# One visit of transposes per expert instead of two in a two-layer decoder trunk

## The reference

```python
xt = v.reshape(-1, d)                       # 512 tokens x 1024
scores = softmax(xt @ w_router)             # 16 experts in 4 groups
# one group per token (sum of its two best scores), then the two best experts in it
for e in range(16):
    hidden = silu(xt @ w_gate[e]) * (xt @ w_up[e])      # 1024 -> 512
    y = y + combine[:, e:e + 1] * (hidden @ w_down[e])  # 512 -> 1024
```

## Time and profile before

| | |
|---|---|
| median of 3 runs | 1138.19 us (1136.5 to 1138.63) |
| the profiled execution's own time | 1138.1 us |
| its span, first to last instruction | 1135.8 us |
| mean granted TensorE clock | 0.997 |
| busy: PE, DVE, ACT, POOL | 1108.5, 894.3, 750.2, 131.6 us |
| DMA | 286.28 MB, mean 252 GB/s over the span |
| expert loops | about 300 to 530 us and 820 to 1050 us of the span |

### The profile page before, as it was taken

One profiled execution on the slowest core, in us unless ns is written; L12 is line 12 of the kernel. 1 busy time (PEld: TensorE's weight loads), 2 busy tenths in 40 slices (PEclk: granted clock), 3 DMA queues, 4 the chain that ended last, 5 costly groups with the idle time before them and its releaser, 6 DMA issues.

```text
span 1135.8 us, 16852 instructions
## 1 busy us (share of the span) xinstructions
PE 1108.5 (98%) x5722; PEld 886.3 (78%) x5722; DVE 894.3 (79%) x1226; ACT 750.2 (66%) x957; POOL 131.6 (12%) x91
## 2 busy tenths in 40 slices
PE   9999999999999999999999999999999999999996
PEld 7888877767888888888788865766888888888785
DVE  6483488358999999999876479638999999999886
ACT  7383322347778787878655469446787878888665
POOL 0000000001212122120000000001221212121000
PEclk9999999999999999999999999999999999999999
DMA  9473222425999999999761310423999999999632
GB/s 367 170 286 149 84 75 81 179 111 210 364 379 375 381 370 387 375 384 376 286 230 46 112 38 20 167 97 136 336 376 380 380 379 370 389 374 387 258 141 74
DMA packets 50595, 286.28 MB, mean 252 GB/s; under 512 B 9321, under 2 KB 9597, under 8 KB 21358
## 3 DMA queue, kind: packets, MB, share of 16 engines
q1 hardware_dynamic: 37086, 250.93, 57.8%
q0 software_dynamic: 13456, 34.65, 8.3%
HBM read 271.38 MB, written 30.41 MB: 266 GB/s over the span
## 4 chain that ended last, share of the span: by engine, by line
PE 84%; DVE 8%; ACT 4%; DMA 2%; issue 1%; SPq 0%; DVEq 0%; ACTq 0%; POOLq 0%
PE psum L568 79%; PE psum L939 2%; DVE arena L2662 2%; ACT whi L1384 2%; DMA arena<-vscr,cur 1%; DVE arena L2675 1%; PE psum L980 1%; DVE wlo L1946 1%; DMA h<-x_dram 1%; DVE wlo L1942 1%; ACT ahi L1384 1%; PE psum L850 1%; DVE h L2496 0%; DVE h L2503 0%; DVE arena L2148 0%
## 5 line engine op out<-in xcount | busy, mean ns | idle before, releaser
L1942 DVE TENSOR_TENSOR wlo<-raw,whi 128x2048 fp32r<-128x2048 f32 x200 | 456.2, 2289 | 69.5 <-ACT whi L1384 58.7
L568 PE MATMUL psum<-whi,ahi 128*128 128x512 f32 x1088 | 434.9, 401 | 4.8 <-ACT ahi L1384 4.3
L568 PE MATMUL psum<-wlo,ahi 128*128 128x512 f32 x1088 | 423.6, 391 | 0.8 <-DVE wlo L1946 0.8
L568 PE MATMUL psum<-whi,alo 128*128 128x512 f32 x1088 | 418.3, 391 | 0.0
L1384 ACT ACTIVATE whi<-raw 128x2048 fp32r<-128x2048 f32 x200 | 382.8, 1915 | 48.5 <-PE psum L568 48.5
L568 PEld LDWEIGHTS psum<-whi,ahi 128*128 128x128 f32 x1088 | 204.8, 188 | 51.7 <-issue 6.9
L568 PEld LDWEIGHTS psum<-whi,alo 128*128 128x128 f32 x1088 | 204.3, 188 | 43.7
L568 PEld LDWEIGHTS psum<-wlo,ahi 128*128 128x128 f32 x1088 | 205.0, 189 | 40.2 <-DVE wlo L1946 1.3
L1384 ACT ACTIVATE arena<-psum 128x512 f32<-128x512 f32 (+3 forms) x150 | 83.3, 565 | 105.6 <-PE psum L568 74.7
L1384 ACT ACTIVATE ahi<-psum 128x512 fp32r<-128x512 f32 x146 | 82.1, 593 | 87.9 <-PE psum L939 39.2
L2770 POOL DMA_INDIRECT arena<-vscr,cur x32 | 69.5, 2173 | 386.0 <-DVE cur L2382 370.7
(11 more groups left out here) (222 smaller groups left out, 899.7 us busy)
## 6 DMA issues: line engine op xcount, KB each, us to landing
raw<-w_moe_dram SPq DMA_DIRECT2D x192, 1024.0 KB, 8.7
raw<-w_dense_dram SPq DMA_DIRECT2D x34, 1024.0 KB, 8.5
yscr<-arena POOLq DMA_DIRECT2D x2, 4096.0 KB, 24.2
arena<-yscr SPq DMA_DIRECT2D x6, 1024.0 KB, 7.0
vscr<-arena POOLq DMA_DIRECT2D x8, 512.0 KB, 2.9
h<-x_dram SPq DMA_DIRECT2D x4, 512.0 KB, 7.7
arena<-w_proj_dram POOLq DMA_DIRECT2D x2, 1024.0 KB, 6.2
arena<-yscr SPq DMA_DIRECT2D x4, 512.0 KB, 4.3
```

The source lines that it names most:

```text
L568: return nc.tensor.matmul(o, l, r, start=start, stop=stop, **kw)
L1942: tt(wlo[:, b % SPL, :], raw[:, b % RAW, :], halves(whi[:, b % SPL, :]), ALU.subtract).then_inc(lo_ready, 1)
```

## The change

PE's step e becomes: gate product of e, `hid_T(e-1)`, `x_T(e+1)`, `index(e+2)`, up product of e, `down(e-1)`. Steps 0 and 15 keep their PE order. `xcols` alternates between the two column ranges by parity, since the rows of e+1 are now split while the up product still reads those of e. ACT splits chunk b+4 before `silu`, and does `x_hi(e+1)` right behind `hid_hi(e-1)`, before chunk b+5. DVE makes `onehot(e+2)` at the head of the step, `x_lo(e+1)` and `index(e+2)` right behind `hid_lo(e-1)`, before chunk b+5, and `hid(e)` behind chunk b+6. POOL's and SP's programs are unchanged.

```diff
--- before.py
+++ after.py
@@ -283,9 +283,9 @@
             for s, n in zip(s_sc, SC_LOADS):
                 eng.wait_ge(s, n * (layer + 1))
 
-        def xcols(e):
-
-            return slice(2 * P, 3 * P) if isinstance(e, int) and e == 1 else slice(0, P)
+        def xcols(par):
+
+            return slice(2 * P, 3 * P) if par else slice(0, P)
 
         def halves(t):
 
@@ -941,9 +941,9 @@
                                 area(AR_XGS[par], D)[:, kt * P:(kt + 1) * P], ident)
                         last.then_inc(m["xt"], 1)
 
-                def up(e, b, e6, bank):
-
-                    xc = xcols(e)
+                def up(par, b, e6, bank):
+
+                    xc = xcols(par)
                     for i in range(2):
                         pe.wait_ge(lo_ready, e6 + (b + i + 1))
                         s = (b + i) % SPL
@@ -1019,22 +1019,24 @@
 
                 def step(e, b, e6, nxt, prev=True, nx2=True):
 
+                    par = 1 - nxt[0] if nxt else LAST % 2
                     if prev:
                         pe.wait_ge(m["xlo"], 2 * e + 2)
                         pe.wait_ge(m["silu"], e)
-                        up(e, b, e6, 0)
+                        up(par, b, e6, 0)
+                        hid_T(e - 1)
                     else:
                         up_first(b)
+                    if nxt:
+                        x_T(e + 1, *nxt)
+                    if prev and nx2:
+                        index(e + 2)
                     if prev:
-                        hid_T(e - 1)
                         pe.wait_ge(m["hid"], e)
                     else:
-                        x_T(e + 1, *nxt)
                         pe.wait_ge(m["pe"], 5)
-                    up(e, b + 2, e6, 1)
-                    if prev and nxt:
-                        x_T(e + 1, *nxt)
-                    if nx2:
+                    up(par, b + 2, e6, 1)
+                    if not prev:
                         index(e + 2)
                     if prev:
                         down(e - 1, b + 4, e6)
@@ -1678,10 +1680,10 @@
                     copy(ahi[:, 0:4, P:2 * P],
                          PS[6][:, :].rearrange("p (a b) -> p a b", a=4)).then_inc(m["hhi"], 1)
 
-                def x_hi(e):
+                def x_hi(e, par):
                     for half in range(2):
                         act.wait_ge(m["xt"], 2 * e + (half + 1))
-                        copy(ahi[:, half * 4:half * 4 + 4, xcols(e)],
+                        copy(ahi[:, half * 4:half * 4 + 4, xcols(par)],
                              PS[4 + half][:, :].rearrange("p (a b) -> p a b", a=4))\
                             .then_inc(m["xhi"], 1)
 
@@ -1694,7 +1696,7 @@
                         .then_inc(m["ou"], 1)
 
                 proj_copy(layer, 5, 2)
-                x_hi(0)
+                x_hi(0, 0)
 
                 def step(e, b, e6, prev=None, nx=True):
                     split(b + 2, e6)
@@ -1702,16 +1704,16 @@
                     if prev is None:
                         proj_copy(layer, 6, 3)
                         split(b + 4, e6)
-                        x_hi(e + 1)
+                        x_hi(e + 1, 1)
                         silu(e, b, e6)
                         split(b + 5, e6)
                         return
+                    split(b + 4, e6)
                     silu(e, b, e6)
-                    split(b + 4, e6)
                     hid_hi(e - 1)
+                    if nx:
+                        x_hi(e + 1, prev[0])
                     split(b + 5, e6)
-                    if nx:
-                        x_hi(e + 1)
                     split(b + 6, e6)
                     result(e - 1, 0, b + 4, e6, *prev)
                     split(b + 7, e6)
@@ -2390,10 +2392,10 @@
                     ts(cur[:, 2 + par:3 + par], v["idx"][:, bass.ds(e * 2 + 1, 1)], FAR, None,
                        ALU.add).then_inc(m["cw"], 1)
 
-                def x_lo(e):
+                def x_lo(e, par):
                     for half in range(2):
                         dve.wait_ge(m["xhi"], 2 * e + (half + 1))
-                        w = (slice(None), slice(half * 4, half * 4 + 4), xcols(e))
+                        w = (slice(None), slice(half * 4, half * 4 + 4), xcols(par))
                         tt(alo[w], PS[4 + half][:, :].rearrange("p (a b) -> p a b", a=4),
                            halves(ahi[w]), ALU.subtract).then_inc(m["xlo"], 1)
 
@@ -2426,36 +2428,38 @@
                 ts(flag[:, layer:layer + 1], v["cnt"][:, 0:1], SLOTS + 0.5, None, ALU.is_gt)\
                     .then_inc(m["flg"], 1)
                 token_weights()
-                x_lo(0)
+                x_lo(0, 0)
 
                 loaded = []
 
                 def step(e, b, e6, nxt, prev=None, nx=True):
+                    if nxt and prev is not None:
+                        onehot(e + 2)
                     split(b + 2, e6)
                     if prev is None:
                         onehot(e + 2)
                         split(b + 3, e6)
                         split(b + 4, e6)
-                        x_lo(e + 1)
+                        x_lo(e + 1, 1)
                         split(b + 5, e6)
                         hid(e, b, e6)
                         index(e + 2, *nxt)
                         return
                     split(b + 3, e6)
-                    if nxt:
-                        onehot(e + 2)
-                    if prev:
-                        split(b + 4, e6)
-                        hid_lo(e - 1)
-                        target(e - 1, *prev)
-                        split(b + 5, e6)
-                    hid(e, b, e6)
+                    split(b + 4, e6)
+                    hid_lo(e - 1)
+                    target(e - 1, *prev)
                     if nx:
-                        x_lo(e + 1)
+                        x_lo(e + 1, prev[0])
                     if nxt:
                         index(e + 2, *nxt)
-                    split(b + 6, e6)
-                    if not nx:
+                    split(b + 5, e6)
+                    if nx:
+                        split(b + 6, e6)
+                        hid(e, b, e6)
+                    else:
+                        hid(e, b, e6)
+                        split(b + 6, e6)
                         loaded.append(over_flag(dve, layer))
                         hid_lo(e)
                     split(b + 7, e6)
```

## The result

The changed kernel takes 1152.69 us in the median (1151.88 to 1153.70), the kernel before 1138.10 beside it: ratio 1.0136, 95% interval 1.0123 to 1.0148. That is 14.6 us slower, against 16 forecast, inside the range.

The account below looks back on a forecast made before the run. TensorE (PE), busy 98% of the span, was taken to bound the kernel. 1138.1 + 11.3 (wait) + 3.4 (clock) + 2.1 (late gathers) - 0.6 (merged visit) = 1154.3, forecast 1154 us, range 1148 to 1163.

Parts of the forecast that it names:

- The wait in step 1: Step 1 of each layer: PE reaches `x_T(2)` before the gather of expert 2 lands; together +11.3 us.
- The clock: Behind the new waits in step 1 of each layer, PE's granted clock falls to half: 2 x 1.7 = +3.4 us.
- Late gathers in the loop: In the loop, gathers' cover shrinks to 0.5 us and a few in layer 1 land late: +2.1 us.
- Rival 1: The loop's gathers become the bound, late on every second expert: +7 to +13 in place of +2.1; chance 0.15.
- The merged visit: Steps 1 to 14 of each layer: one visit of transposes instead of two saves 0.02 us each, -0.6 us over 28.
- The two rules: DMA page: gather lands after 3.2 us, stall 1.0 us a layer; clock page: +3.4 us by its rule, without it 0.

Follow-up runs that it names:

- The early feed: Changed kernel with what releases the gather of expert 2 (`onehot(2)`, `index(2)`, DVE's write of `cur`) moved early as well; 1136.23 us, ratio 0.9986.
- the filler: Changed kernel with 105 small matmuls, results unused, between `hid_T(0)` and `x_T(2)` in step 1, where PE waits; 1147.75 us, ratio 1.0089.
- 50 fillers: Changed kernel with 50 small matmuls, results unused, between `hid_T(0)` and `x_T(2)` in step 1; 1153.46 us, ratio 1.0134.
- the later `cur`: Changed kernel with the early `index(2)`, and DVE's write of `cur` put behind the split b+5 instead of in front; 1164.73 us, ratio 1.0249.
- two visits and a later `hid`: Kernel before, both visits of transposes kept, with DVE's `hid(e)` moved behind the split b+6; 1135.48 us, ratio 0.9980.

## Why the prediction was right

**The wait in step 1.** Right in place, cause and size: +11.27 said, +11.71 in the trace. The gather started where it did, 1.2 us ahead of `hid_T(0)`, and took 7.9 and 8.1 us (7.8 said). The early feed takes the wait away and, with the half clock behind it, 16.5 us.

**The clock.** Right that it falls; the term was too small: 2 x 1.7 said, 2.97 + 1.95 measured, and 4.9 when the filler takes it away. I took the one row, where PE had restarted just as the clock fell and half clock lasted 3.4 us. Here it fell while PE stood and went on for 6.4 and 4.2 us of work (with 50 fillers for 3.4 and 3.3); why it lasted longer, and not the same in the two layers, no run shows.

**Late gathers in the loop.** The cover, 10.92 us, was right to the digit. The term (+2.1) was not there: landings were 9.0 to 10.5 us instead of 9.9 to 12.0. It is a term of chance: two other executions of the same loop had one of 11.5 and one of 11.6, and the later `cur` shows what it costs when the cover is gone. Rival 1 didn't come true here, but the medians are only 0.7 to 1.0 us under the cover. The kernel with two visits and a later `hid` has landings of 9.6 to 11.0, medians 10.0, with the scatter behind the down product as before, so the scatter's distance from the gather need not be the reason; why they shortened stays open.

**The merged visit.** -0.6 said, -0.79 measured over the two loops, and for another reason. The one visit costs as much as the two did (1.52 and 1.51 us), and the kernel with two visits gains more than this from DVE's `hid` behind the split b+6 (1.43 us over the same steps), which I had put at nothing because I took the loop for free of waits. The earlier trace rows can't show a wait that only a weight load has.

**The sum.** 1138.1 + 11.7 + 4.9 - 0.8 = 1153.9; the median is 1152.69. That the total came so near is partly luck: the clock's term was 1.5 too small and the late gathers' 2.1 too large. In the profiled pair, 1.5 us of the difference is the half clock near 190 us that one of the two had.

**The two rules.** The gather took 7.9 us beside full queues and PE waited 6.15. By the Trainium skill's "DMA: Bandwidth & Descriptors" (section "Anatomy of one DMA — SWDGE (gpsimd) path") the estimate was 3.2 us and a wait of 1.5; the measurement decides against it here. The clock stayed at 1.00 when useless matmuls filled the wait; the Trainium skill's "TensorE: Matmul & The Clock Gate" (Part 1, "What's actually happening"), by which activity releases the throttled state, agrees.

## What to carry to other kernels

When work is moved forward, ask of each operand when it is produced in the first and last turns as well: a loop whose steady state has cover can stall in a written-out first step whose producer didn't move. A stall of several us on PE costs its length and then a stretch of half-speed work behind it, here 40% more than the wait alone. And before merging visits to an engine, compare the visit's length with the sum of its instructions: where they agree, there is no switching cost to save.

## What was not expected of the hardware

The same 2.21 us of idleness near 188 to 190 us stands in all nine profiles, in front of the same matmul. In three of them (the kernel before, the early gather, the two visits with later `hid`) the clock then fell to 0.50, with a mean of 0.83 over 188 to 198 us; in six it stayed at 1.00. So an idle stretch of this length costs 1.7 us or nothing from one execution to the next, and the spans of single profiles differ by that much without any change of code. The waits of 6 us brought the fall each time.

This bears on the medians too, though only profiled executions have a timeline. Of eleven runs of the two visits with later `hid`, five had a mean clock of 0.996 and took 1136.5 to 1137.0 us, six had 0.997 or 0.998 and took 1134.2 to 1135.5. Beside them 26 of 29 runs of the kernel before had 0.996 or 0.997. So a median can move by 1 us or more with the number of runs in which the clock fell; that this fall is what parts them is likely and not shown.

The gather of expert 2 in layer 1, with loads in flight each time, took 7.6, 8.1 and 10.7 us (before, after, and with 50 fillers).
